# x2's prompt tiles transposed by VectorE and DMA in place of TensorE, the samples' tile a step later, tile 6 of the first block back on TensorE

## The reference, cut

```python
def swiglu(x, wg, wu, wd):
    return (silu(x @ wg) * (x @ wu)) @ wd          # 1024 -> 2816 -> 1024

def trunk_layer(x, ...):
    x = layer_norm(ALPHA * x + 0.5 * swiglu(x, f1...))      # its result is called x1
    z = x @ w_in + b_in                                     # 1024 -> 2560, split in five
    u = a_val * sigmoid(a_gate)
    ua = silu(layer_norm(causal_depthwise31(u) + b_dw_a))
    ub = g_b * causal_depthwise3(g_c * b_val)
    x = layer_norm(ALPHA * x + concat(ua, ub) @ w_o + b_o)  # x2
    return layer_norm(ALPHA * x + 0.5 * swiglu(x, f2...))
```

## Time and profile before

| what | value |
|---|---|
| median of 3 runs | 1208.29 us (1206.06 to 1209.5) |
| profiled execution, its own time | 1206.11 us |
| its span on the slowest core (core 2) | 1204.2 us |
| spans of the cores | 1196.5 to 1204.2 us, clock 0.993 to 0.996 |
| TensorE busy | 1176.2 us (98%) |
| VectorE, ScalarE, GpSimd busy | 616.0, 235.7, 190.8 us |

### The profile page before, as it was taken

How to read it: one execution, slowest core, us unless ns; L and a number is a source line. 1 busy time by engine, 2 the same in 40 slices (tenths; PEclk the granted TensorE clock), 3 DMA queues, 4 the chain that set the end, 5 groups by cost and what they waited for, 6 DMA issues and landing times.

```text
span 1204.2 us, 20136 instructions; the slowest of 8 cores (1196.5 to 1204.2 us)
## 1 busy us (share of the span) xinstructions
PE 1176.2 (98%) x7128; PEld 638.2 (53%) x7128; DVE 616.0 (51%) x932; ACT 235.7 (20%) x437; POOL 190.8 (16%) x302
## 2 busy tenths in 40 slices
PE   8999999989999999999799999999999999999997
PEld 4544444445555666654355555545444466666443
DVE  2223228756555565718886556564736532222366
ACT  3211100011222235310011222235320011111000
POOL 0111102301101023312111100123212110000111
PEclk9999999999999999999899999999999999999999
DMA  8799987977666569894457666569963254443033
GB/s 278 116 200 149 150 145 175 192 185 125 112 109 109 130 133 177 182 210 135 136 145 125 114 107 113 132 139 172 196 164 121 91 106 84 72 71 88 21 110 105
DMA packets 78290, 163.26 MB, mean 136 GB/s; under 512 B 9136, under 2 KB 35952, under 8 KB 76896
## 3 DMA queue, kind: packets, MB, share of 16 engines
q0 software_dynamic: 28352, 76.07, 40.3%
q1 hardware_dynamic: 49840, 85.91, 24.2%
HBM read 206.41 MB, written 32.37 MB: 198 GB/s over the span
## 4 chain that ended last, share of the span: by engine, by line
PE 92%; DVE 3%; DMA 2%; issue 1%; POOL 1%; SPq 1%; ACT 0%; DVEq 0%; ACTq 0%; POOLq 0%
PE ps L577 50%; PE ps L641 22%; PE ps L738 11%; PE ps L1021 5%; PE ps L856 1%; DMA sb_RW<-xta 1%; PE ps L659 1%; DMA xscr<-sb_tq 1%; PE ps L434 1%; PE ps L990 1%; PE ps L962 1%; DVE sb_stt L478 1%; DVE sb_xb L503 1%; DVE sb_xr L474 0%; POOL sb_mv L482 0%
## 5 line engine op out<-in xcount | busy, mean ns | idle before, releaser
L577 PE MATMUL ps<-sb_xB,sb_ring 128*128 128x352 bf16 (+1 forms) x2112 | 319.6, 310 | 0.0
L577 PE MATMUL ps<-sb_xA,sb_ring 128*128 128x512 bf16 (+1 forms) x1472 | 311.6, 370 | 2.3 <-DVE sb_ring L1197 1.9
L584 DVE TENSOR_TENSOR sb_hT<-sb_sg,ps 128x352 bf16<-128x352 f32 (+3 forms) x224 | 129.6, 579 | 344.4 <-PE ps L577 321.6
L641 PE MATMUL ps<-sb_RW,sb_hT 128*128 128x512 bf16 x1364 | 297.5, 381 | 0.0
L577 PEld LDWEIGHTS ps<-sb_xB,sb_ring 128*128 128x128 bf16 x2112 | 205.9, 98 | 106.9 <-issue 1.1
L582 ACT ACTIVATE sb_sg<-ps 128x352 f32<-128x352 f32 (+3 forms) x224 | 113.8, 508 | 597.6 <-PE ps L577 479.4
L577 PEld LDWEIGHTS ps<-sb_xA,sb_ring 128*128 128x128 bf16 x1472 | 142.9, 98 | 157.4 <-issue 4.7
L641 PEld LDWEIGHTS ps<-sb_RW,sb_hT 128*128 128x128 bf16 x1364 | 133.5, 98 | 161.6 <-issue 2.9
L372 POOL DMA_DIRECT2D sb_ring<-wgu x84 | 46.7, 555 | 462.3 <-PE ps L577 400.2
L474 DVE SCALAR_TENSOR_TENSOR sb_xr<-sb_xr,ps 128x1024 f32<-128x1024 f32 x47 | 57.2, 1217 | 86.2 <-PE ps L641 78.1
L482 POOL TENSOR_SCALAR sb_mv<-sb_mv 128x1 f32<-128x1 f32 (+1 forms) x50 | 43.5, 870 | 363.1 <-DVE sb_mv L480 355.8
(11 more groups left out here) (102 smaller groups left out, 609.3 us busy)
## 6 DMA issues: line engine op xcount, KB each, us to landing
sb_ring<-wgu POOLq DMA_DIRECT2D x84, 512.0 KB, 6.9
sb_RW<-wd POOLq DMA_DIRECT2D x33, 512.0 KB, 10.8
sb_wring<-win POOLq DMA_DIRECT2D x40, 256.0 KB, 5.3
sb_RW<-uscr SPq DMA_DIRECT2D x128, 67.0 KB, 5.1
sb_xr<-xp SPq DMA_DIRECT2D x16, 512.0 KB, 7.8
x1s<-sb_xr SPq DMA_DIRECT2D x16, 512.0 KB, 3.8
sb_xr<-x1s SPq DMA_DIRECT2D x16, 512.0 KB, 9.7
x2s<-sb_xr SPq DMA_DIRECT2D x16, 512.0 KB, 6.9
```

The lines of the kernel that those rows point to most:

```text
L577: ins = e.matmul(bank(bk, n), lhsT=ring[:, s, c:c + 128], rhs=xcol(k, tok0, n), start=(k == 0), stop=(k == KC - 1))
L584: P.op("dve", lambda e: e.tensor_tensor(out=hT[:, f, l0:l0 + n], in0=sg[:, q, :n], in1=bank(bu, n), op=ALU.mult), reads=[("sg", q)] + pst( ...
L641: ins = e.matmul(ps[:n, (yb + h) * 512:(yb + h + 1) * 512], lhsT=hT[:, f, l0:l0 + n], rhs=wd[:, f, h * 512:(h + 1) * 512], start=(f == 0), ...
```

## The change

In `down`, a tile that waits for its transposition on TensorE carries the step in which it came, and is taken up only two steps later. So the samples' tile is transposed after tile 13's pass and not after tile 12's. In the first block tile 6 no longer goes by `xmove`; it waits with tile 7 for the place in the first mixing stage where tile 7 was transposed. In unit E, `xpose` of tile i-5 is replaced by `xmove`; ahead of it `land_moves(1)` issues the read-backs of all but the last move, so a read-back comes two moves behind its write. The last ones are issued by `four`, behind the units. The samples' x2 tile stays on TensorE.

```diff
-        def land_moves():
-            while moves:
+        def land_moves(keep=0):
+            while len(moves) > keep:
                 moves.pop(0)()
...
-                while pend:
-                    xpose(*pend.pop(0), tb())
+                while pend and pend[0][2] <= i - 2:
+                    xpose(*pend.pop(0)[:2], tb())
...
-                        if t < 16 and i < len(tl) - 1:
+                        if t < 16 and i < len(tl) - (2 if b == 0 else 1):
                             xmove(t, c)
                             return []
-                        return [(t, c)]
+                        return [(t, c, i)]
...
-                    pend.extend(fin(*late))
+                    pend.extend((t_, c_, i) for (t_, c_, _) in fin(*late))
...
                 for k in at(i, 5, True):
-                    xpose(tl[k], xbs[k], ((3, 3, 3, 7), (3, 6, 3, 7))[par][k])
+                    land_moves(1)
+                    xmove(tl[k], xbs[k])
...
-            side.append((lambda: [xpose(*p, cb5()) for p in pend], 1.0))
+            side.append((lambda: [xpose(*p[:2], cb5()) for p in pend], 1.0))
...
             def four():
+                land_moves()
```

## The result

The changed kernel took 1231.7 us (median of the undisturbed runs; two of its four were disturbed and are left out here and below in the same way), the kernel before 1207.2: a ratio of 1.020, 95% interval 1.018 to 1.022. The forecast was 1209, its range ended at 1223.

A forecast was written before the change was run, and what follows sets the result against it. It took TensorE, working without a gap in both mixing stages, as the bound. Savings of 18.2 us against losses of 18.9 gave +0.7 on the median of 1208.29, so 1209 us, range 1194 to 1223.

The forecast's parts named there:

- tile 6 and samples' tile: Start of first mixing stage and second down projection: TensorE's waits go, saving 7.0 us and 4.0 us.
- transpositions off TensorE: Mixing stages: sixteen x2 tiles lose their transpositions on TensorE, 0.45 us each, saving 7.2 us.
- the 2.0: End of both mixing stages: VectorE's added copies delay the next matmul groups, 2.0 us lost, ends 0 and 5.
- the 18.9: Sum of forecast losses: 12.3 us second mixing stage, 4.6 first mixing stage, 2.0 at the stages' ends.
- The same in the first mixing stage: First mixing stage: x1 load behind the writes of two tiles lands late, 4.6 us lost, ends 0.3 and 14.
- half of 6.6: First mixing stage: the load of x1 queues behind one set of small writes still under way, half of 6.6 us.
- The second mixing stage: Late load of x1 holds VectorE's multiply and then TensorE: 12.3 us lost, ends 3.8 and 19.
- the wait at the output projection: Second mixing stage: load landing at 854 makes TensorE wait 10.4 us, and 1.95 us of clock.
- the wait at the last tile's transposition: Behind the second down projection: TensorE, coming earlier, waits 3.8 us for VectorE, with 1.0 us taken off for the clock.
- A: The forecast: waits for two loads of x1 eat the savings; 1204 to 1214 us, chance 0.40.
- B: Slower: small writes hardly get through, the gating load lands late; 1216 to 1228 us, say 1219, chance 0.28.
- C: Faster: the transfers hide in gaps and loads land at the lower ends; 1194 us, chance 0.32.

The follow-up runs named there:

- e1: The kernel before with only the down projections' part of the change (tile 6, samples' tile); x2 tiles stay on TensorE: 1197.6 us.
- e12: The changed kernel with the x2 tiles neither transposed nor moved by any engine: 1192.9 us.
- e7: The changed kernel with VectorE's transpositions of the x2 tiles, but without their writes and read-backs: 1200.5 us.
- e8: The changed kernel with the writes of the x2 tiles, but without their read-backs: 1226.0 us.
- e14: The changed kernel with the x2 transfers replaced by equal writes of constant data in SyncE's queue, waiting for nothing and waited for by nobody: 1213.8 us.
- e6: The changed kernel with each x2 tile's four writes in whole rows of 2048 bytes in place of pieces of 512 bytes: 1223.2 us.
- e4: The changed kernel with four tq buffers in place of two: 1231.2 us.
- e13: The changed kernel with the x2 transfers replaced by equal writes of constant data in ScalarE's queue, waiting for nothing and waited for by nobody: 1201.4 us.

## Why the prediction was wrong, step by step

The parts in us, from medians:

| step | forecast | measured | from |
|---|---|---|---|
| tile 6 and samples' tile | -11.0 | -9.6 | e1 |
| transpositions off TensorE | -7.2 | -4.7 | e12 against e1 |
| VectorE's transpositions | in the 2.0 | +7.6 | e7 against e12 |
| writes | in the 18.9 | +25.5 | e8 against e7 |
| read-backs | in the 18.9 | +5.7 | after against e8 |

The three together are 38.8 us of loss against 18.9 forecast; the gains are 14.3 against 18.2.

**The step that failed** is "The same in the first mixing stage", 4.6 us (ends 0.3 and 14). Against e12 the stage lost 17.8 us (289.0 - 271.2), 5.6 being forecast with half of the stages' end. e7, e14 and e8 split it: 4.4 for VectorE, 0.4 for the writes' traffic and place, 13.5 for the real writes' waits and later issue (and -0.5 for the read-backs). Two terms of the sum were too small. The first is the load at 478.01. I had it land 3.3 us later than the 12.5 of the earlier trace rows ("half of 6.6"), at 15.8 us, and TensorE wait 3.6 us with 1.0 of clock. It took 22.02, the wait was 9.65 and the clock cost 2.1 (4.62 for 2.55), 11.7 us in place of 4.6:
```profile
460.30 22.02 DMA sb_xr<-x1s
...
483.22 4.62 PE L577 MATMUL ps<-sb_xB,sb_ring 128*128 128x352 bf16 x16 [9.65 <-DVE sb_hT L584]
```
The four writes ahead of it are issued at 456.02, 4.3 us before it, because VectorE turns that tile only at 454.70. The free writes of e14 are out at 451.84, and the load takes 15.0 us there, 14.5 with no writes (e7). With whole rows (e6) it takes 16.27. The `tq` wait ahead of it costs nothing here: without it (e4) TensorE waits 10.5 us for the same load.

The second term is the `tq` waits at the stage's end, which I named ("more if a copy waits until the write of the tile two back has landed") and priced at 2.0 us for both stages. From the chain of waits, where the earlier trace rows had none:
```profile
516.24 10.06 DMA xscr<-sb_tq
526.40 1.25 DVE sb_tq L447
...
529.30 14.33 DMA xscr<-sb_tq
```
Such a write had 8.4 us in the earlier trace rows, and in the kernel before the last four tiles are turned 2.8 us apart (L434 at 504.97, 507.79, 510.62 and 513.50), so two back is 5.7 us, and turning, issuing and landing take 11.4 together (1.24, 1.78 and 8.4): the wait could have been worked out, at some 6 us. VectorE waited 6.67 there, and TensorE 4.1. With four buffers (e4) the stage is 5.0 us shorter, but the second down projection loses 5.1: SyncE then stands at the read-backs for the same landings, ahead of the load of xp.

**A step that was missing**: the second down projection lost 7.4 us against e12 (87.8 and 80.4). The read-backs that `four()` lands stand in SyncE's queue ahead of the load of xp, and VectorE waited 20.3 us for it. The list of what the change puts into that queue stopped at the loads of x1.

**The second mixing stage** was sized right: 13.2 us against e12 (290.6 - 277.4), 13.3 forecast (12.3 and half of 2.0); the wait at the output projection is 11.0 us, 10.4 forecast, and the clock 1.84 (5.29 - 3.45), 1.95 forecast. Its working was wrong twice, in opposite directions, so the hit is in part luck. Moved by the 8.2 us that the stage starts later, the load should have been issued at 843 and taken 19.1 us; it was issued at 861.46 and took 9.51. The issue is late by the `tq` wait of 8.0 us and by 6.6 us of slow issues (8.4 in place of 1.78); most of the other 3.7 is that VectorE comes to a's fourth tile at 843.6 even without its wait (843.61 in e4), 3.4 us later in the stage than my 832. None of this sets the landing, as the table over all runs shows. By stages, VectorE has 2.6 of the 13.2 us, the free writes in SyncE's queue 7.8, what the real ones add 5.0, and the read-backs -2.2.

**Right:** tile 6 (6.5 of 7.0); the wait at the last tile's transposition (3.6 of 3.8 in e1; in the changed kernel, where xp is late, 4.75 of the 6.9 us stand at the samples' tile already); and that the transpositions are worth single microseconds, 4.7 for all sixteen tiles, where the 275 ns of the Trainium skill (TensorE: Matmul & The Clock Gate, Part 4: PE-mode transpose) would have made 35. **Mis-sized:** the samples' tile, 4.0, which gave 1.6 by the stages (9.2 less 7.6), by the clock behind that wait and 1.3 untraced; and the 7.2 us, which the 0.45 us of the earlier trace rows price rightly as work, but of which a third went into waits.

**The rivals.** A's mechanism was there, but its 1204 to 1214 us were not. B comes nearest: slower, through late small writes. Its place was not: the wait in the second mixing stage is 11.0 us, not its 14.3, and the first has 11.7 with the clock in place of its 8. Its range ended at 1228, since it had the writes delay the two x1 loads only. Its mechanism, small writes that hardly get through, is half of it: e13's free writes hurt nobody. C falls with e8.

**Still open:** e14 doesn't part the real writes' waits from their later issue; the read-backs' traffic was never run by itself; why the landing in the second mixing stage doesn't follow the issue; and why whole rows (e6) shorten the load's landing in the first mixing stage and not in the second (landed at 250.2 there).

## What to carry to other kernels

When work is moved from an engine to transfers, write down the queue that issues them and everything behind them in it, up to the loads of the next stage, and price each issue, landing and buffer from the rows of the busiest stretch, not the quiet one. A first experiment with the same transfers, free of waits, in another queue tells in one run whether the bytes cost. Don't judge a load by when it is issued: look at when it lands. And take the parts of a change apart: here one part was worth 9.6 us and the other lost 31 to 34.

## What the runs showed of the hardware

The issue of a write of 64 KB in SyncE's queue takes 0.45 us at the median of the changed kernel and up to 3.59, with earlier writes still under way; the load at 827.23 in e14 held the sequencer for 7.36 us:
```profile
827.23 7.36 SPq L416 DMA_DIRECT2D sb_xr<-x1s  x1
```
SyncE's queue had 26.5 and 25.7% of the DMA engines' time in e13 and e14 with very different contents, but it isn't a fixed share: the kernel before has 21.8 and the changed kernel 19.2% from 815 to 850, and the changed kernel 29.8% from 450 to 500.
